# A two-block diffusion layer on one core: decay's scan behind the short convolution, root tables called ahead of the last squares, three row sums, three weight chunks and one load elsewhere

## Chip, cores and metric

One core of a Trainium2 chip runs the whole program in one launch. The time is the device time of one execution in microseconds; three executions of the kernel before took 1831.81, 1833.35 and 1838.54, median 1833.35.

## The reference

A latent sequence `x` of 256 tokens and a context of 256 tokens, 1024 features each, in float32, go through three layers: one block with a gated delta rule, a short convolution and a Fourier branch, then a block with retention and mLSTM, and a block with windowed attention. Each has a SwiGLU network with 2816 hidden features, and every norm is modulated by vectors that come from `c` through a 1024 x 6144 matrix.

```
mod = silu(c) @ w_mod + b_mod                 # six vectors per layer, for x and for the context
h   = rmsnorm(x) * gain * (1 + scale) + shift
qkv, z, ba, sc, fn = split(h @ w_in)
qkv = silu(conv3(qkv)); q, k = l2norm(q), l2norm(k)
g   = cumsum over a chunk of  -exp(a_log) * softplus(alpha + dt_bias)     # "decay"
o   = gated_delta(q, k, v, beta, g)           # both directions, context then latent
y   = gates * (o_branch, sc_branch: sb * conv3(scc * sx), fourier_branch)
x   = x + g1 * (y @ w_o);  x = x + g2 * swiglu(modulate(rmsnorm(x)))
# layer 2: retention and mLSTM mixer;  layer 3: attention, its mod from row sums of ada_w
```

## The kernel before

Tokens lie along the free axis and features along the partitions. Every weight product is made in three passes: ScalarE copies a weight tile to `wh` (the high half, L1685), VectorE or GpSimd subtracts to `wl` (the low half, L2219 and L824), and TensorE multiplies `wh` with the high and the low half of the activations and `wl` with the high half (L949 to L951). A latent tile (256 tokens) is 24 products, a joint tile (512 tokens) 24 longer ones.

**Order.** Each engine runs a list written out by hand, and all follow one plan (`make_plan`): the sequence of 1 MB weight chunks that SyncE loads into three slots `raw`, and of PSUM tiles that take eight banks in turn. SyncE issues chunk n only when chunk n-3 has been read or split (L802 and the waits ahead of it). Only three split tiles (`wh`, `wl`) exist, so `ahead(key)` on ScalarE, VectorE and GpSimd splits at most three tiles in front of the one that TensorE uses. Anything put in front of a split on an in-order engine delays it.

**Decay.** After qkv and the 128 columns `ba`, the stages z, scc, sx, sb and fn follow, four tiles each. ScalarE and VectorE make softplus of `ba` together (`softplus_act`, `softplus_dve`), VectorE makes gain and sign (two instructions from L2377), then `scan_dve` (L751): eight scans over 128 tokens, two directions by four chunks. They give `RM`, which TensorE transposes after the fn tiles. Beside the stages from scc on runs `l2norm`: ScalarE squares a key or query, TensorE sums and ScalarE roots it (L1853), VectorE inverts (L2387), TensorE spreads (L1071), VectorE multiplies (L2392). TensorE meets a spread after every second tile. In the sx stage VectorE also makes the short convolution (L2358 to L2360, L2418), after clearing its pads (L2405).

**Norms.** `behind` squares a residual tile (L1699) as soon as it has been added, while TensorE makes later tiles; after the last square `root` (L1705) takes the square root of the mean, VectorE inverts (L2278), TensorE spreads (L1044) and VectorE and ScalarE scale and shift. Silu, exp, sqrt and the like lie in different tables of ScalarE; a load (ACT_TABLE_LOAD) precedes the first activation that needs another one. The norms are a1, a2 (first layer), b1 (also the first block's final norm, L1986), b1c, b2, c1 and c2; the mLSTM output has a norm of its own per head (L2035).

**Mod.** 48 chunks of modulation weights are multiplied on TensorE (L1003) in groups placed by `mod(count)`, each group followed one call later by its transposes (L1013). In the recurrence of the gated delta rule (four steps s) a group of two comes at level 2 and another behind level 6. Further groups stand behind the last gate tile (2), between `ydn` and `wo` (1) and at the start of ffn0 (3), in front of the spread of a2. The third layer's modulation is not multiplied: 32 units of rows (`rboth`, `rlat`) are loaded beside the chunks of ffn1, and VectorE sums each against `cond` in two instructions (L2265, `row_sums`); the slot is held until the sum is there. `row_chunk` says beside which chunk a unit stands: in 1 to 7, out 0 to 3, in 8 to 15, out 4 to 7, in 16 to 21, out 8 to 10. ffn1's low halves are all made on GpSimd.

**ffn.** For j = 0 to 21 there are two tiles `fa`, `fb` (gate and value), silu on ScalarE, product and split on VectorE; after 8, 16 and 22 of them come eight output tiles `fo`. In ffn0 step 0 is loaded ahead (`load` ... `use`), and its tiles are made in a pair that follows the norm feature tile by feature tile.

Of the kernel before, what the change touches and what calls it, by code (L numbers as in the profile page):

```python
# [30 lines left out]
ALU = mybir.AluOpType  # L31
# [5 lines left out]
KD = D // P  # L37
# [47 lines left out]
def row_chunk(nm, what, i):  # L85

    if nm != "1" or (what, i) == ("in", 0) or (what, i) == ("out", 11):
        return None  # L90
    at = [("in", x) for x in range(1, 8)] + [("out", x) for x in range(4)]
    at += [("in", x) for x in range(8, 16)] + [("out", x) for x in range(4, 8)]
    at += [("in", x) for x in range(16, 22)] + [("out", x) for x in range(8, 11)]
    return at.index((what, i))

# [10 lines left out]
def make_plan():  # L106
# [77 lines left out]

    def rows_mod(c):

        if c is not None:
            chunk("rboth" if c < BOTH else "rlat", c % BOTH)
            chunks[-1]["unit"] = c
# [7 lines left out]
    def ffn(name, early=None):  # L197
        for g, (k0, nk) in enumerate(GROUPS):
            if g == 2 and early:
                norm(early)  # L200
            for j in range(k0, k0 + nk):
                if j == 0:
                    load("ffn_in" + name, 0, [("fa" + name, 0), ("fb" + name, 0)])
                    if name == "0":
                        mod(3)
                    if name == "1":
                        mod(0)
                    spread({"0": "a2", "1": "b2", "2": "c2"}[name])
                    if name == "0":
                        mod(0)  # L210
                    use([("fa" + name, 0), ("fb" + name, 0)])
                else:
                    split("ffn_in" + name, j, [("fa" + name, j), ("fb" + name, j)])
                if g == 2 and early and j == k0:
                    spread(early)
                rows_mod(row_chunk(name, "in", j))
# [41 lines left out]
    for s in range(NC + 1):  # L258
# [36 lines left out]
        for n in two:  # L295
            add("Y", n, LV - 1)
        mod(2)
        for n in two:
# [15 lines left out]
    load("w_o", 0, [("wo", 0), ("wo", 1)])  # L314
    mod(1)
    use([("wo", 0), ("wo", 1)])
# [140 lines left out]
def build(nc, dram, out):  # L457
# [283 lines left out]

    def scan_dve(dve, src, dst, op, start, done):


        V = nc.vector
        for d in range(2):
            rr = slice(32 * d, 32 * d + 32)
            turn = 1 if d == 0 else -1
            for c in range(NC):
                tk = slice(CH * c, CH * c + CH)  # L750
                ins = V.tensor_tensor_scan(dst[rr, tk][:, ::turn], CA("ones")[rr, :], src[rr, tk][:, ::turn], start,  # L751
                                           ALU.mult, op)
        ins.then_inc(sem(done), 1)
        dve.wait_ge(sem(done), 1)

# [157 lines left out]
    def _(pe):  # L913
# [464 lines left out]
        for m in range(KD):  # L1378
# [3 lines left out]
            plain(("ydn", m), lambda k: w[:, 512 * k + o:512 * k + o + P], lambda k: oacc[:, k, :], 4, L)  # L1382
        mod()
        for m in range(KD):
# [287 lines left out]
    def _(act):  # L1672
# [24 lines left out]
        def square(name, k, nm_res, dst=sqh):  # L1697
            for r, cc in nm_res:
                ins = A(dst[:, k, cc], r[:, k, :], ACT.Square)  # L1699
            ins.then_inc(sem(name + "_sq"), 1)  # L1700

        def root(name):
            rows_n = group_rows(name)
# [8 lines left out]
        def behind(name, m, of, nm_res, dst=sqh):  # L1712

            for k in ((m - 2,) if m < KD - 1 else (m - 2, m - 1, m)):
                if k >= 0:
                    evacuated(act, *of(k))
                    square(name, k, nm_res, dst)

        def shift(name, nidx, nm_res):

            lay, sec = nidx // 2, 3 * (nidx % 2)
            for k in range(KD):
                act.wait_ge(sem(name + "_mul"), k + 1)
                for r, cc in nm_res:
# [23 lines left out]
        def ffn(nm, halves, early=None, after=None):  # L1748
            c0 = T - L * halves
            for g, (k0, nk) in enumerate(GROUPS):  # L1750
# [22 lines left out]
                for m in range(KD):  # L1773
# [6 lines left out]
                    if g == 2 and after == "b1":  # L1780
                        for k in ((m - 2,) if m < KD - 1 else (m - 2, m - 1, m)):
                            if k >= 0:
                                evacuated(act, "fo0", 2 * KD + k)
                                final_squares(k)
# [44 lines left out]
        for what in ("z", "scc", "sx", "sb", "fn"):  # L1829
            for i in range(4):  # L1830
# [8 lines left out]
                if what == "z":  # L1839
                    full(act, "z", i)  # L1840
                    free(A(zsave[:, i, :], bank("z", i)[:, 0:L], ACT.Silu), "z", i)
                elif what == "scc":
                    full(act, "scc", i)
# [127 lines left out]
        for k in range(KD):  # L1971
# [3 lines left out]
            A(mgh[:, k, :], merged[:, k, :], ACT.Copy).then_inc(sem("mg_hi"), 1)  # L1975
        mod()
        for m in range(KD):
# [130 lines left out]
        for s in range(NC):  # L2108
# [18 lines left out]
            full(act, "MD", s)  # L2127
            free(A(den[:], bank("MD", s)[:, 0:P], ACT.Abs), "MD", s)
        mod()
        act.wait_ge(sem("mout_sum"), 2)  # L2130
# [79 lines left out]
    def _(dve):  # L2210
# [40 lines left out]

        def row_sums(c):

            if c is None:
                return
            n = unit_at[c]
# [119 lines left out]
        softplus_dve(dve, link, "dsp", r, tmp)  # L2376
        link(V.scalar_tensor_tensor(r[:, 3, :], r[:, 0, :], 0.0, r[:, 3, :], ALU.max, ALU.add))  # L2377
        evacuated(dve, "ba", 0)
        link(V.tensor_scalar(r[:, 0, :], r[:, 3, :], tiny[0:64, 0:1], -1.0, ALU.mult, ALU.mult))
        scan_dve(dve, rows[0:64, 0, :], RM[0:64, :], ALU.add, 0.0, "RM_ready")  # L2380

# [13 lines left out]
        for what in ("z", "scc"):  # L2395
            for i in range(4):
                ahead(what, i)
                if i % 2:
                    if what == "scc":
                        l2norm(i // 2)  # L2400

        pads = [cb[:, i % 3, 0:4 * (GRID + 1) + 1] for i in range(4)]
        dve.wait_ge(sem("conv_done"), 12)
# [3 lines left out]
        for i in range(4):  # L2407
# [12 lines left out]
            if i % 2:  # L2420
                l2norm(2 + i // 2)
        for i in range(4):
            ahead("sb", i)
            full(dve, "sb", i)
            free(V.tensor_tensor(scy[:, i, :], bank("sb", i)[:, 0:L], scy[:, i, :], ALU.mult), "sb", i)
            if i % 2:
                l2norm(4 + i // 2)
        for i in range(4):
            ahead("fn", i)
# [180 lines left out]
        for m in range(KD):  # L2610
            if m == 2:
# [7 lines left out]
                            ALU.subtract).then_inc(sem("mg_split"), 1)  # L2619
        mod()  # L2620
        for m in range(KD):
# [570 lines left out]
```

## Time and profile before

| | us |
|---|---|
| median of three runs | 1833.35 (1831.81 to 1838.54) |
| the profiled execution | 1837.42 |
| its span | 1835.6 |
| TensorE busy | 1720.0 (94%), 14308 products |
| VectorE / ScalarE / GpSimd busy | 938.8 / 733.9 / 592.2 |
| HBM read | 259.44 MB, 142 GB/s over the span |
| mean granted clock | 0.969 |

The profile is one execution of the program. Busy time is the union of an engine's instructions; register, branch and DMA-issuing instructions are not in it. The chain is followed back from the last instruction to what released each one. The granted clock is TensorE's, as a share of full speed.

### The profile page before, as it was taken

The page shows a single profiled execution, that of the slowest core. Times are in us where ns is not written, and L with a number is a line of the kernel's source. Part 1 is how long each engine was busy: PE and PEld are TensorE (multiplying, and loading weights), DVE is VectorE, ACT ScalarE, POOL GpSimd, SP SyncE. Part 2 cuts the span into 40 slices and gives each one's busy share as a digit, 9 for nine tenths or more (in the row PEclk, how much of TensorE's full clock was granted, in tenths as well). Part 3 has the DMA queues.
Part 4 walks back from the last instruction along what each step waited for, and adds up shares of the span by engine and source line. Part 5 has one row for each costly group of instructions (what it writes and reads, how often), then busy time and mean ns, then how long its engine had stood idle before and what let it go on. Part 6 is the DMA issues. An engine that isn't in the chain of part 4 may idle for free.

```text
span 1835.6 us, 33658 instructions
## 1 busy us (share of the span) xinstructions
PE 1720.0 (94%) x14308; PEld 1508.0 (82%) x14308; DVE 938.8 (51%) x1723; ACT 733.9 (40%) x1267; POOL 592.2 (32%) x302
## 2 busy tenths in 40 slices
PE   4997998999989999899999799999999989989998
PEld 1787997888889999697798577888888777689998
DVE  1758126576443333543487626554554546744333
ACT  2463522232345464431555324212212245744443
POOL 0245322121133443214233024444445312134443
PEclk8999999999999999999999899999999989999999
DMA  8433343332464544423220323434545432035553
GB/s 320 190 137 115 116 161 128 141 146 96 169 236 178 185 180 165 157 93 139 81 92 25 116 74 110 152 124 181 186 185 198 153 119 92 2 104 195 184 184 116
DMA packets 37876, 262.66 MB, mean 143 GB/s; under 512 B 4192, under 2 KB 4320, under 8 KB 8416
## 3 DMA queue, kind: packets, MB, share of 16 engines
q1 hardware_dynamic: 37728, 260.51, 38.6%
q8 instruction: 114, 1.87, 0.4%
q14 instruction: 34, 0.28, 0.0%
HBM read 259.44 MB, written 1.05 MB: 142 GB/s over the span
## 4 chain that ended last, share of the span: by engine, by line
PE 82%; DVE 8%; DMA 3%; ACT 3%; issue 2%; POOL 1%; SPq 0%; DVEq 0%; ACTq 0%; POOLq 0%
PE ps L949 20%; PE ps L951 19%; PE ps L950 19%; PE ps L1003 2%; DMA raw<-in_mod 2%; PE ps L978 2%; PE ps L967 1%; PE ps L968 1%; PE ps L969 1%; POOL wl L824 1%; PE ps L1309 1%; PE ps L1104 1%; PE ps L1655 1%; PE ps L1633 1%; PE ps L1027 1%
## 5 line engine op out<-in xcount | busy, mean ns | idle before, releaser
L824 POOL TENSOR_TENSOR wl<-raw,wh 128x1024 fp32r<-128x1024 f32 (+1 forms) x213 | 519.4, 2442 | 995.2 <-ACT wh L1685 995.2
L949 PE MATMUL ps<-h_hi,wh 128*128 128x256 f32 (+1 forms) x1696 | 546.9, 322 | 7.5 <-POOL wl L824 5.6
L950 PE MATMUL ps<-h_lo,wh 128*128 128x256 f32 (+1 forms) x1696 | 542.1, 320 | 0.0
L951 PE MATMUL ps<-h_hi,wl 128*128 128x256 f32 (+1 forms) x1696 | 542.0, 320 | 0.0
L1685 ACT ACTIVATE wh<-raw 128x1024 fp32r<-128x1024 f32 (+1 forms) x330 | 341.7, 1040 | 397.2 <-PE ps L951 256.8
L949 PEld LDWEIGHTS ps<-h_hi,wh 128*128 128x128 f32 x1696 | 324.1, 191 | 34.3 <-POOL wl L824 7.0
L951 PEld LDWEIGHTS ps<-h_hi,wl 128*128 128x128 f32 x1696 | 324.0, 191 | 22.7
L950 PEld LDWEIGHTS ps<-h_lo,wh 128*128 128x128 f32 x1696 | 324.2, 191 | 22.5
L2219 DVE TENSOR_TENSOR wl<-raw,wh 128x1024 fp32r<-128x1024 f32 (+1 forms) x117 | 146.5, 1252 | 210.6 <-ACT wh L1685 210.5
L949 PE MATMUL ps<-gh,wh 128*128 128x256 f32 (+1 forms) x528 | 170.1, 322 | 0.4 <-POOL wl L824 0.4
L951 PE MATMUL ps<-gh,wl 128*128 128x256 f32 (+1 forms) x528 | 168.8, 320 | 0.0
L950 PE MATMUL ps<-gl,wh 128*128 128x256 f32 (+1 forms) x528 | 168.7, 319 | 0.0
L2265 DVE CUSTOM_DVE_ANT_0 cjunk<-raw,cond,small 128x1024 f32<-128x1024 f32 x64 | 139.3, 2213 | 1.9 <-ACT cond L1768 1.9
L2329 DVE TENSOR_TENSOR sil<-ps,sil 128x256 f32<-128x256 f32 (+1 forms) x66 | 33.9, 514 | 194.7 <-PE ps L951 192.3
L949 PEld LDWEIGHTS ps<-gh,wh 128*128 128x128 f32 x528 | 101.0, 191 | 10.0 <-issue 2.0
L951 PEld LDWEIGHTS ps<-gh,wl 128*128 128x128 f32 x528 | 100.9, 191 | 7.1
L950 PEld LDWEIGHTS ps<-gl,wh 128*128 128x128 f32 x528 | 101.0, 191 | 6.9
L1764 ACT ACTIVATE sil<-ps 128x256 f32<-128x256 f32 (+1 forms) x66 | 30.0, 454 | 152.9 <-PE ps L951 150.6
L845 POOL TENSOR_TENSOR d_Xc<-d_Ac,const 128x256 f32<-128x256 f32 x40 | 31.9, 814 | 136.6 <-DVE d_Ac L2514 101.2
L2345 DVE SCALAR_TENSOR_TENSOR res_l<-ps,mods,res_l 128x256 f32<-128x256 f32 x72 | 34.6, 480 | 59.4 <-PE ps L951 59.4
L1003 PE MATMUL ps<-raw,small 128*32 128x256 f32 x768 | 53.5, 419 | 9.9 <-DMA raw<-in_mod 9.5
L1104 PE MATMUL ps<-h_hi,wh 128*128 128x512 f32 (+1 forms) x96 | 40.0, 417 | 17.6 <-DVE h_lo L2305 17.6
(441 smaller groups left out, 2577.0 us busy)
## 6 DMA issues: line engine op xcount, KB each, us to landing
raw<-in_ffn_in SPq DMA_DIRECT2D x66, 1024.0 KB, 4.8
raw<-in_mod SPq DMA_DIRECT2D x48, 1024.0 KB, 5.1
raw<-in_ffn_out SPq DMA_DIRECT2D x24, 1024.0 KB, 4.8
raw<-in_w_in SPq DMA_DIRECT2D x16, 1024.0 KB, 4.8
raw<-in_rlat SPq DMA_DIRECT2D x16, 1024.0 KB, 4.8
raw<-in_w_gate SPq DMA_DIRECT2D x12, 1024.0 KB, 4.8
raw<-in_w_ab SPq DMA_DIRECT2D x12, 1024.0 KB, 4.9
raw<-in_ffn_out SPq DMA_DIRECT2D x12, 768.0 KB, 4.2
```

The source lines that it names most:

```text
L824: nc.gpsimd.tensor_tensor(wl[e % SPLIT][:, 0:entries[e]["words"]], part(e), wh[e % SPLIT][:, 0:entries[e]["words"]].bitcast(F32), ALU.subt ...
L949: nc.tensor.matmul(b[:, cols], wh[e % SPLIT][:, w], xh(k), start=(k == 0), stop=False)
L950: nc.tensor.matmul(b[:, cols], wh[e % SPLIT][:, w], xl(k), start=False, stop=False)
L951: ins = nc.tensor.matmul(b[:, cols], wl[e % SPLIT][:, w], xh(k), start=False, stop=(k == nk - 1))
L978: ins = nc.tensor.matmul(b[:, 0:cols], w(k), rhs(k), start=(k == 0), stop=(k == nk - 1))
L1003: ins = nc.tensor.matmul(b[32 * j:32 * j + 32, 0:256], small[:, o:o + 32], w[:, 256 * k:256 * k + 256], start=(a == 0 and k < 4), stop=(a ...
L1104: nc.tensor.matmul(o, wh[e % SPLIT][:, w], xh(k), start=(k == 0), stop=False)
L1685: A(wh[e % SPLIT][:, 0:x["words"]], part(e), ACT.Copy).then_inc(hi_ready, 1)
L2219: V.tensor_tensor(wl[e % SPLIT][:, 0:entries[e]["words"]], part(e), wh[e % SPLIT][:, 0:entries[e]["words"]].bitcast(F32), ALU.subtract).th ...
L2265: V.tensor_tensor_reduce(cjunk[:, e, :], w, cond[:, v, :], 1.0, S("bmod")[:, 96 + o:97 + o], ALU.mult, ALU.add, mods[:, 2, o, v:v + 1]).th ...
L2329: free(V.tensor_tensor(sil[:, j % 4, c0:T], bank("fb" + nm, j)[:, c0:T], sil[:, j % 4, c0:T], ALU.mult), "fb" + nm, j)
L2345: ins = V.scalar_tensor_tensor(r[:, m, :], bank("fo" + nm, KD * g + m)[:, cc], mods[:, lay, 40 + m, v:v + 1], r[:, m, :], ALU.mult, ALU.add)
```

## The change

It moves work between places and adds seven small activations; what is computed stays the same.

1. *Decay*: the end of softplus and the two instructions behind it stand behind the scc stage; the scans of direction 0 behind the sx stage, those of direction 1 behind the sb stage. Only the last scan signals and is waited for.
2. *Root tables*: `call_root` takes a square root of one column into a spare column, so that the table is in: behind the last silu of z, ahead of the last square of each norm made by `behind` (a2, b2, c1, c2) and of b1, and behind the last denominator of mLSTM.
3. *Row sums*: the units of out 8, 9 and 10 become second units of in 17, 19 and 21.
4. *Mod chunks*: the group behind level 6 has three chunks instead of two in steps s = 1, 2, 3; the group between `ydn` and `wo` is gone, and that of ffn0 has one chunk instead of three.
5. *Load*: step 1 of ffn0 is loaded right behind step 0, ahead of the mod group, and ScalarE calls its first split inside the shift of a2, at feature tile 4.

```diff
 def row_chunk(nm, what, i):
-    if nm != "1" or (what, i) == ("in", 0) or (what, i) == ("out", 11):
-        return None
+    if nm != "1":
+        return ()
     at = [("in", x) for x in range(1, 8)] + [("out", x) for x in range(4)]
     at += [("in", x) for x in range(8, 16)] + [("out", x) for x in range(4, 8)]
-    at += [("in", x) for x in range(16, 22)] + [("out", x) for x in range(8, 11)]
-    return at.index((what, i))
+    at += [("in", x) for x in (16, 17, 17, 18, 19, 19, 20, 21, 21)]
+    return [u for u, place in enumerate(at) if place == (what, i)]
...
                     load("ffn_in" + name, 0, [("fa" + name, 0), ("fb" + name, 0)])
                     if name == "0":
-                        mod(3)
+                        load("ffn_in0", 1, [("fa0", 1), ("fb0", 1)])
+                        mod(1)
...
         for n in two:
             add("Y", n, LV - 1)
-        mod(2)
+        mod(3 if s else 2)
...
     load("w_o", 0, [("wo", 0), ("wo", 1)])
-    mod(1)
     use([("wo", 0), ("wo", 1)])
...
+        def call_root():
+            A(tiny[:, 300 + roots[0]:301 + roots[0]], eps, ACT.Sqrt)
+            roots[0] += 1
...
             for k in ((m - 2,) if m < KD - 1 else (m - 2, m - 1, m)):
                 if k >= 0:
+                    if k == KD - 1:
+                        call_root()
                     evacuated(act, *of(k))
                     square(name, k, nm_res, dst)
...
             for k in range(KD):
+                if (name, k) == ("a2", 4):
+                    ahead("fa0", 0)
                 act.wait_ge(sem(name + "_mul"), k + 1)
...
                     free(A(zsave[:, i, :], bank("z", i)[:, 0:L], ACT.Silu), "z", i)
+                    if i == 3:
+                        call_root()
...
             free(A(den[:], bank("MD", s)[:, 0:P], ACT.Abs), "MD", s)
+        call_root()
         mod()
...
         softplus_dve(dve, link, "dsp", r, tmp)
-        link(V.scalar_tensor_tensor(r[:, 3, :], r[:, 0, :], 0.0, r[:, 3, :], ALU.max, ALU.add))
-        evacuated(dve, "ba", 0)
-        link(V.tensor_scalar(r[:, 0, :], r[:, 3, :], tiny[0:64, 0:1], -1.0, ALU.mult, ALU.mult))
-        scan_dve(dve, rows[0:64, 0, :], RM[0:64, :], ALU.add, 0.0, "RM_ready")
...  # the four z tiles and the four scc tiles with two norms
+        link(V.scalar_tensor_tensor(r[:, 3, :], r[:, 0, :], 0.0, r[:, 3, :], ALU.max, ALU.add))
+        evacuated(dve, "ba", 0)
+        link(V.tensor_scalar(r[:, 0, :], r[:, 3, :], tiny[0:64, 0:1], -1.0, ALU.mult, ALU.mult))
...  # pads, the four sx tiles with the convolution and two norms
+        scan_dve(dve, rows[0:64, 0, :], RM[0:64, :], ALU.add, 0.0, "RM_ready", (0,))
         for i in range(4):
             ahead("sb", i)
...
+        scan_dve(dve, rows[0:64, 0, :], RM[0:64, :], ALU.add, 0.0, "RM_ready", (1,))
         for i in range(4):
             ahead("fn", i)
```

## Rows read from the trace of the kernel before

**Rows 1.** The page: busy time (share of the span) and instructions; the chain by engine.
```profile
PE 1720.0 (94%) x14308; PEld 1508.0 (82%) x14308; DVE 938.8 (51%) x1723; ACT 733.9 (40%) x1267; POOL 592.2 (32%) x302
...
PE 82%; DVE 8%; DMA 3%; ACT 3%; issue 2%; POOL 1%; SPq 0%; DVEq 0%; ACTq 0%; POOLq 0%
```
**Rows 2.** Stretches: length, busy of PE, PEld, DVE, ACT, POOL, granted clock, DMA share, GB/s.
```profile
143.00:150.00 7.00, 0.00 (x0) 0.00 (x0) 6.95 (x9) 1.79 (x3) 4.06 (x2) 0.84 0.41 150
150.00:156.00 6.00, 5.62 (x31) 5.62 (x32) 3.31 (x6) 0.00 (x0) 0.00 (x0) 0.62 0.00 0
156.00:176.00 20.00, 17.90 (x159) 16.83 (x157) 18.90 (x24) 8.36 (x12) 12.95 (x6) 1.00 0.33 110
...
547.00:551.00 4.00, 4.00 (x23) 4.00 (x22) 1.42 (x2) 0.77 (x1) 2.46 (x1) 0.57 0.45 137
...
1444.00:1452.00 8.00, 5.39 (x30) 4.04 (x29) 5.49 (x9) 2.81 (x6) 2.64 (x2) 0.98 0.61 230
1452.00:1456.00 4.00, 4.00 (x12) 3.09 (x12) 0.31 (x2) 0.00 (x0) 1.99 (x1) 0.62 0.64 213
...
289.00:485.00 196.00, 178.18 (x3194) 159.83 (x3193) 123.53 (x334) 64.62 (x137) 42.05 (x44) 0.97 0.34 126
```
**Rows 3.** Timeline of VectorE: start, us, instruction, count.
```profile
139.91 2.52 DVE L2379 TENSOR_SCALAR rows<-rows,tiny 64x512 f32<-64x512 f32 x1
142.47 6.87 DVE L751 TENSOR_TENSOR_SCAN RM<-const_all,rows 32x128 f32<-32x128 f32 x8
...
175.05 0.95 DVE L2387 RECIPROCAL l2c<-l2c 128x128 f32<-128x128 f32 x1
```
**Rows 4.** The scan's line: duration in ns, min/median/max.
```profile
L751 DVE TENSOR_TENSOR_SCAN RM<-const_all,rows x8: 385/389/2484, 142.5 to 149.0; 32x128 f32<-32x128 f32 x8
```
**Rows 5.** Timeline of ScalarE at a2, ffn0, b1 and b2: in brackets the idle time before.
```profile
531.47 0.42 ACT L1699 ACTIVATE sqh<-res_l 128x256 f32<-128x256 f32 x1 [2.26 <-DVE res_l L2624]
531.90 1.28 ACT L1705 ACT_TABLE_LOAD   x1
533.20 0.36 ACT L1705 ACTIVATE rc<-ps,small 64x128 f32<-64x128 f32 x1
...
543.15 1.04 ACT L1685 ACTIVATE wh<-raw 128x1024 fp32r<-128x1024 f32 x1
...
738.88 0.42 ACT L1745 ACTIVATE sqh<-res_l 128x256 f32<-128x256 f32 x1 [0.75 <-DVE res_l L2345]
...
1098.77 0.37 ACT L1705 ACTIVATE rc<-ps,small 128x128 f32<-128x128 f32 x1 [0.55 <-PE ps L1027]
```
**Rows 6.** Chain of waits in mLSTM's head norm: start, us, what.
```profile
1035.94 3.24 PE ps L1003 x32
```
**Rows 7.** Chain of waits in the last output group of ffn1.
```profile
1444.20 4.22 DMA raw<-in_ffn_out
```
**Rows 8.** VectorE, 1362 to 1436 us: groups, busy, mean ns, idle before; durations.
```profile
L2265 DVE CUSTOM_DVE_ANT_0 cjunk<-raw,cond,small 128x1024 f32<-128x1024 f32 x14 | 29.7, 2154 | 0.0
L2329 DVE TENSOR_TENSOR sil<-ps,sil 128x512 f32<-128x512 f32 x6 | 4.2, 692 | 33.8 <-PE ps L951 33.8
...
L2265 DVE CUSTOM_DVE_ANT_0 cjunk<-raw,cond,small x14: 1274/1278/3421, 1365.3 to 1428.5; 128x1024 f32<-128x1024 f32 x14
```
**Rows 9.** Chain of waits in steps 1 and 2 of the recurrence.
```profile
362.91 1.86 PE ps L1003 x32
...
397.76 7.98 DMA raw<-in_mod
...
405.78 1.07 PE ps L1003 x16
```
**Rows 10.** Issues of mod chunks, 398.5 to 399.3 us: time to landing.
```profile
DMA to landing us min/median/max: 8.0/9.4/10.8
```
**Rows 11.** Chain of waits at the start of ffn0.
```profile
536.15 0.65 PE ps L1044 x4
```
**Rows 12.** What TensorE waited for, 530 to 552 us: total, times, longest.
```profile
PE ps L949 <- POOL wl L824: 1.8, 1, 1.8
```

More of the change, by code:

```diff
@@ L183, in mod, with rows_mod @@
         mods[0] += count
-    def rows_mod(c):
-        if c is not None:
+    def rows_mod(units):
+        for c in units:
             chunk("rboth" if c < BOTH else "rlat", c % BOTH)
@@ L211, in ffn @@
                     use([("fa" + name, 0), ("fb" + name, 0)])
+                elif (name, j) == ("0", 1):
+                    use([("fa0", 1), ("fb0", 1)])
                 else:
@@ L740, in softplus_dve, with scan_dve @@
         link(V.tensor_tensor(r[:, 3, :], r[:, 3, :], tmp, ALU.add))
-    def scan_dve(dve, src, dst, op, start, done):
+    def scan_dve(dve, src, dst, op, start, done, directions=(0, 1)):
         V = nc.vector
-        for d in range(2):
+        for d in directions:
             rr = slice(32 * d, 32 * d + 32)
@@ L752, in scan_dve @@
                                            ALU.mult, op)
-        ins.then_inc(sem(done), 1)
-        dve.wait_ge(sem(done), 1)
+        if directions[-1] == 1:
+            ins.then_inc(sem(done), 1)
+            dve.wait_ge(sem(done), 1)
     HALF = (slice(0, 64), slice(64, P))
@@ L1382, in _ @@
             plain(("ydn", m), lambda k: w[:, 512 * k + o:512 * k + o + P], lambda k: oacc[:, k, :], 4, L)
-        mod()
         for m in range(KD):
@@ L1700, in square @@
             ins.then_inc(sem(name + "_sq"), 1)
+        roots = [0]
+        def call_root():
+            A(tiny[:, 300 + roots[0]:301 + roots[0]], eps, ACT.Sqrt)
+            roots[0] += 1
         def root(name):
@@ L1782, in ffn @@
                             if k >= 0:
+                                if k == KD - 1:
+                                    call_root()
                                 evacuated(act, "fo0", 2 * KD + k)
@@ L1975, in _ @@
             A(mgh[:, k, :], merged[:, k, :], ACT.Copy).then_inc(sem("mg_hi"), 1)
-        mod()
         for m in range(KD):
@@ L2128, in _ @@
             free(A(den[:], bank("MD", s)[:, 0:P], ACT.Abs), "MD", s)
+        call_root()
         mod()
@@ L2250, in mod, with row_sums, unit_sums @@
                                                     ALU.add, ALU.mult))
-        def row_sums(c):
-            if c is None:
-                return
+        def row_sums(units):
+            for c in units:
+                unit_sums(c)
+        def unit_sums(c):
             n = unit_at[c]
@@ L2619, in _ @@
                             ALU.subtract).then_inc(sem("mg_split"), 1)
-        mod()
         for m in range(KD):
```

## The prediction

> **What bounds the kernel now.** I read the page's busy shares and its chain first: TensorE is busy 94% of the span and carries 82% of the chain [rows 1]. What can be won is only time in which TensorE waits or runs at half clock, so the next view was the granted clock by stretch, and then, at every place the diff touches, what ended TensorE's wait. The reader is to see two costs there: the wait itself, and the stretch behind it. From 143 to 150 us TensorE does nothing; from 150 to 156 us it works at a granted clock of 0.62, part of it therefore at the lower level of 1.2 GHz; from 156 on it is 1.00 again [rows 2]. The same pair stands at 1444 to 1456 us.
>
> The profiled execution took 1837.4 us, 1.8 more than its span; the median of the three runs is 1833.35, 4.1 lower. I take every saving from the trace and subtract it from the median, since the waits below are orders of work and not disturbances.
>
> **Part 1, the scan of decay.** Before, VectorE finishes softplus, then gain and sign (2.52 us), then eight scans (6.87), ending at 149.34, and only then inverts the first key norm, for which TensorE waits from just before 143 until past 150, about 7.5 us [rows 2, 3]. A scan by itself takes 0.39 [rows 4]; the two long ones, and the 2.52 of an instruction of 64 rows, fall beside GpSimd's subtractions. In the new order norm 0 is inverted while TensorE still makes the last scc tile, norm 1 as soon as it is rooted (144.3), and then follow the two decay instructions (about 3 with one collision) and the three memsets (1.6), so that the convolutions begin near 150 and not at 156.4. The wait of 7.5 goes, and with it the low clock behind it, 6 us at 0.62, about 2 us.
>
> What is late next is VectorE itself. Its four convolutions and two inversions run from 156.4 to 176.0 (18.9 of 20 us busy [rows 2]), and TensorE waits there for norm 3, inverted at 175.05 to 176.0 [rows 3]. So this 19.6 us chain and not the 9.5 us sets the gain. Started at 150 it ends at 169.6 if it loses as much to GpSimd as before (gain 6.4), and near 166 if half of its four collisions of 2.0 each go (gain 10; TensorE's own work since 143 would end about there). I take 7.5. The scans come back in two halves of 4 x 0.39 = 1.6, up to 2 x 2.1 more when blocked, one before the sb multiplies and one before the fn norms. There TensorE works through two tiles of 3 us between any two norms and does not need RM until the transposes behind fn, so they cost nothing; if that cover is gone, 1.6 to 3.7 each.
>
> Trainium skill, "SBUF — State Buffer", section "Who interferes with whom": a VectorE instruction with two SBUF inputs is blocked for the whole of a GpSimd instruction that reads SBUF. The trace agrees for the scan (0.39 alone, up to 2.48 [rows 4]). By that rule every collision stays where GpSimd runs, which speaks for the 6.4 end.
>
> **Part 2, root tables called ahead.** At a2 the last square is followed by a load of 1.28 and then the root [rows 5]. At b2, where the root's table is already in, the root starts 0.55 behind its square (the wait for TensorE's sum), against 1.31 here. A call put behind square 6 runs in ScalarE's wait of 2.3 for the last tile, so a2, c2 and c1 gain 1.31 - 0.55 = 0.76 each. At b1 ScalarE idles only 0.75 before square 7; call and load (1.5) push the squares back 0.7 of the 1.3 saved: 0.6. In mLSTM's head norm the load stands on the chain, TensorE's mod chunks behind it run partly at half clock (3.24 us for two chunks [rows 6], 1.9 elsewhere), and the second chunk's landing limits them; I take 1.9, between 1.3 (the load) and 2.6 (load and clock). At z the call adds 1.5 us to ScalarE and delays one split that GpSimd, busy back to back, would not take earlier: nothing. At b2 it is a 0.2 us activation in a wait. Parts without a2: 0.76 + 0.76 + 0.6 + 1.9 = 4.0; bounds 2.5 and 5.5.
>
> Trainium skill, "ScalarE: Activation LUTs", section "What ACT_TABLE_LOAD costs": a switch costs 1283 ns and a drain of about 1380 behind it. By that figure each place would give nearly twice as much. The trace shows the root 0.02 us behind the load [rows 5], so nothing of a drain is there to save.
>
> **Part 3, three row sums.** In the last output group of ffn1 a sum on VectorE holds a slot, SyncE issues the next weight chunk only at 1444.20 [rows 7], and TensorE works 5.4 of the 8 us from 1444 (2.6 of waiting), then runs 1452 to 1456 at 0.62 [rows 2], 1.7 more. Sums at out 8 to 10 no longer exist, so both go: 4.3. They are added at in 17, 19 and 21. There 14 sums, seven units in 74 us, so one step of 10.6 each, take 2.15 on average, 4.3 a unit, and in six waits VectorE waits 33.8 us for TensorE, 5.6 a step [rows 8]; a second unit leaves 1.3. The two units' slots come free some 4 us later, which the splits, due a step later, can bear. I take a loss of 0.5: net 3.8, bounds 4.3 and -1.
>
> **Part 4, three mod chunks and one load.** In the recurrence TensorE is 91% busy (178.2 of 196 us) at a granted clock of 0.97 [rows 2]. Two chunks take 1.86 [rows 9], so three more cost 2.8. At s = 2 the w_gate chunk holds a slot until GpSimd's split ends, and three chunks are then issued together: the second lands at 405.74, TensorE waits 0.5 for it and is done with it at 406.85; a third issued at 398 to 399 takes up to 10.8 [rows 9, 10], so it lands at 408.5 to 409.7: 2.3 lost, and half a chance of 1.7 of low clock behind it. At s = 1 and 3 the third slot is free long before. Sum: -2.8 - 2.3 - 0.9 = -6.0 (bounds -3, -9). The chunk taken from between ydn and wo gives nothing back: there ScalarE and VectorE split the merged tiles and TensorE waits anyway.
>
> What it buys is the start of ffn0. Now three chunks stand between the sum of a2 and its spread, which runs at 536.15 [rows 11], and the first tile of step 1 waits 1.8 for its split [rows 12], since ScalarE begins that at 543.15 only behind the shift [rows 5]. It then runs at 0.57 clock, 23 products in the 4 us to 551 [rows 2], so that its second tile starts at about 551. New: root at 532.45 and done at 532.8, inverse (0.95) at 533.8, spread at 533.85, 2.3 earlier, a2's table with it. The split called inside the shift, 1.04 us of ScalarE, makes VectorE wait 0.5. Tiles 0, which closed at 544.8, close at 543.0, step 1 begins at once and at full clock, and its second tile waits until about 546.6 for its own split, which stands behind the silu table (1.28), silu (0.4), the high half (1.04) and the low half (1.2), counted from 542.7: against 551 that is 4.5 gained (bounds 2.5 and 6). Part 4: -1.5.
>
> **The sum.** 7.5 + 4.0 + 3.8 - 1.5 = 13.8 us. From the profiled execution 1823.6; from the median 1819.6, so 1820.
>
> **Rivals.**
> *A. VectorE's port (0.20).* The moved chain is blocked as often as before or more often (decay's two instructions, the first half of the scans now ahead of norm 4), gain 4; and double sums run past the step: a sum takes 1.27 alone and up to 3.42 behind a split [rows 8], so four at 3.0 and 1.4 for the gate products come to 13.4 against 10.6. At in 21 the last gate product is then late, a wait of 2.8 plus a clock fall of 1.7 eats part 3. For it: 18.9 of 20 us busy [rows 2]. Against it: 5.6 us of waiting a step [rows 8]. 13.8 - 3.5 - 4 = 6.3: 1827. The page of the skill named in part 1 states the lock that this works by.
> *B. Slower: the third chunk (0.05).* Place: the end of s = 1, 2, 3. If each time it is the last of three in flight, TensorE loses 0.93 + 2.9 and then a stretch of 6.8 us at half clock, 3.4: 7.2 a time, 21.7 in all against the 19.8 that the other terms give: 1835. It decides against the change from 6.6 us a step on. Against it: only s = 2 has the gate chunk in the slot that counts.
> *C. The call doesn't serve (0.07).* If the squares or copies behind it call for another set, the root still loads and ten loads stand where five stood: part 2 and 0.8 of a2 go, 1 us is added: 1825. Against it: at b2 squares and copies lie between two roots with no load [rows 5].
> *D. More (0.18).* VectorE collides half as often (10), no clock falls at s = 2, ffn0 gives 6: 13.8 + 2.5 + 0.9 + 1.5, about 19: 1815.
>
> **How the numbers follow.** The forecast has 0.50, its own range 1816 to 1824. The five cases put 8 in 10 between 1813 and 1829. A measurement of this kernel tells about 0.5% (9.2 us) from no change, so faster means below 1824.2: most of the forecast, all of D, a quarter of A and a third of C, 0.71; same 0.25; slower 0.04.
>
> **What would show it.** Right: no wait of TensorE at 143, one or two of under 4 us between 155 and 167, the transposes behind fn some 7 us earlier; roots 0.55 behind their last square at a2, c1 and c2; no wait in the last output group of ffn1; a wait of 2 to 3 us on a mod chunk at the end of s = 2 and none at s = 1, 3; no wait for the split of step 1 in ffn0. Wrong: the 7.5 us reappear before norm 3 or at the fn norms; loads stand in front of the roots; in21's products are late; or the recurrence stage is over 8 us longer.

## The result, and the profile after

| kernel | median of its runs, us | mean granted clock |
|---|---|---|
| before | 1833.29 (1828.57 to 1838.54, 6 runs) | profiled 0.969 |
| after | 1818.23 (1811.64 to 1823.54, 6 runs) | 0.974 to 0.981 |

The ratio is 0.9908, 95% interval 0.9885 to 0.9931: 15.1 us less in the medians, where 1820 was forecast (a sum of 13.8 less). The profiled execution took 1813.53 us, at the fast end of its six. Two far slower executions further down, of 2800 and 4243 us, are in no median and no comparison.

The page of the kernel after, busy time and chain by engine, answers to [rows 1]:

```profile
PE 1705.2 (94%) x14306; PEld 1496.4 (83%) x14306; DVE 926.7 (51%) x1722; ACT 734.5 (41%) x1273; POOL 590.4 (33%) x302
...
PE 83%; DVE 7%; DMA 4%; ACT 3%; issue 2%; POOL 1%; SPq 0%; DVEq 0%; ACTq 0%; POOLq 0%
```

Span less TensorE's busy time is its waiting: 115.6 us before (1835.6 - 1720.0), 106.5 after (1811.7 - 1705.2). So of the 23.9 us between the two profiled executions only 9.1 are waits; the other 14.8 are nearly the same products done in less time, at a higher granted clock (0.981 against 0.969). How much of that belongs to the change is seen where next to no part of it acts. Stretches of the same 2146 products, from the gates to mLSTM (columns as in [rows 2]), in the kernel before, the kernel after and a second profile of the kernel after:

```profile
800.00:1026.00 226.00, 218.16 (x2146) 189.14 (x2144) 141.03 (x305) 93.56 (x154) 72.05 (x44) 0.98 0.22 78
```

```profile
790.00:1014.50 224.50, 215.87 (x2146) 186.50 (x2145) 141.08 (x305) 94.87 (x156) 72.09 (x44) 1.00 0.22 78
```

```profile
788.50:1016.00 227.50, 219.63 (x2146) 190.16 (x2144) 141.07 (x305) 94.98 (x156) 72.06 (x44) 0.98 0.22 77
```

The wait is 7.8, 8.6 and 7.9 us, but the length 226.0, 224.5 and 227.5: the clock alone makes 1.5 us either way. The next table therefore has two profiles of the kernel after. Each number is how much earlier (-) or later (+) a stretch ends than it began, against the same TensorE products of the kernel before; the stretch is named by its time there. The last column is the profile of the kernel that has only that part.

| stretch (us of before) | forecast | after | after, 2nd | part alone |
|---|---|---|---|---|
| 0 to 120, nothing changed | 0 | -0.2 | -1.9 | |
| 120 to 182, decay and convolution | -7.5 | -8.0 | -7.9 | -8.0 |
| 182 to 286, up to the recurrence | 0 | +0.3 | +0.6 | +0.6 |
| 286 to 484, recurrence | +6.0 | +2.5 | +4.3 | +3.9 |
| 484 to 530, ydn and wo | 0 | +0.3 | -1.6 | -1.2 |
| 530 to 556, a2 and ffn0's start | -4.5 | -3.6 | -3.6 | -2.8 |
| 734 to 800, b1 | -0.6 | -1.3 | -1.3 | -1.3 |
| 800 to 1026, nothing of weight | 0 | -1.5 | +1.5 | -1.5 |
| 1026 to 1056, head norm | -1.9 | -2.6 | -1.1 | -2.8 |
| 1070 to 1106, b2 | 0 | -0.9 | -0.5 | -0.9 |
| 1440 to 1460, last output group of ffn1 | -4.3 | -4.3 | -4.3 | -4.3 |
| 1460 to 1497, c1 | -0.8 | -2.0 | -0.8 | -0.4 |
| 1600 to 1650, c2 | -0.8 | -1.8 | -1.9 | -1.8 |

(In the last column, the rows up to 286 are decay's kernel, those of the recurrence to ffn0 the chunks', ffn1's the sums', and the other rows from b1 to c2 the tables'. The 0.5 forecast as lost at in 17 to 21 is not there: from 1106 to 1440 the lead changes by 0.0 and by -0.3. What is left out, 1497 to 1600, changes by -0.8 and -0.1, with no wait changed.)

The kernels with one part alone are also each other's control, since most of them have no edit in a given stretch. This is how far such unedited stretches move against the kernel before, and what TensorE waits in them before and after:

| stretch | kernels without an edit there | waiting before, after |
|---|---|---|
| 120 to 182 | -0.5, -0.4 | 12.3, 4.8 |
| 286 to 484 | +1.3, -1.3, -1.7 | 17.8, 19.1 |
| 734 to 800, b1 | -0.6, -0.6, +0.8 | 4.7, 4.1 |
| 1070 to 1106, b2 | 0.1 at most | 5.2, 5.2 |
| 1440 to 1460 | +0.1, +0.1, +0.1 | 2.6, 0.0 |
| 1460 to 1497, c1 | 0.0, +0.3, 0.0 | 6.4, 5.7 |
| 1600 to 1650, c2 | 0.0, +0.2, 0.0 | 5.9, 5.1 |

So a row of the first table is safe as it stands for decay and the output group of ffn1. In the recurrence it is good to some 1.5 us, and of b1's 1.3 a half is there without the edit in two kernels of three. At b1, c1 and c2 the waiting fell by 0.6, 0.8 and 0.8, which is the forecast; what the rows show beyond it, and all of b2's 0.9, is clock.

**Decay.** Stretches of the kernel after, against [rows 2]:

```profile
143.00:150.00 7.00, 7.00 (x65) 6.67 (x64) 6.41 (x9) 2.71 (x5) 5.38 (x3) 1.00 0.44 150
150.00:156.00 6.00, 6.00 (x52) 6.00 (x53) 5.75 (x8) 2.88 (x4) 3.60 (x3) 1.00 0.55 178
156.00:168.00 12.00, 9.91 (x76) 9.17 (x75) 11.58 (x17) 2.68 (x5) 6.00 (x3) 0.86 0.24 89
```

VectorE there, against [rows 3], and what TensorE waits for in 150 to 172:

```profile
144.61 2.53 DVE L2418 SCALAR_TENSOR_TENSOR rows<-rows 64x512 f32<-64x512 f32 x1
...
151.48 2.46 DVE L2437 COPY scy<-cy 128x256 f32<-128x256 f32 x1
...
155.34 2.48 DVE L2380 SCALAR_TENSOR_TENSOR cy<-cb,small,cy 128x259 f32<-128x259 f32 x1
...
158.19 0.95 DVE L2403 RECIPROCAL l2c<-l2c 128x128 f32<-128x128 f32 x1
...
164.71 0.95 DVE L2403 RECIPROCAL l2c<-l2c 128x128 f32<-128x128 f32 x1
...
166.13 3.38 DVE L753 TENSOR_TENSOR_SCAN RM<-const_all,rows 32x128 f32<-32x128 f32 x4
```

```profile
PE ps L1074 <- DVE l2c L2403: 2.1, 1, 2.1
```

TensorE works through 143 to 156 at full clock. The wait left is one of 2.1 us at the spread of norm 2, and a lower clock (0.86) stands behind it: VectorE's chain, 11.6 of 12 us busy, is the bound up to there, as forecast. In the convolutions two of its instructions are blocked for about 2 us (2.46 and 2.48) where before there were four, and it inverts norm 3 at 164.71 instead of 175.05: 10.3 earlier, the forecast's upper end for VectorE, of which TensorE, with its wait at norm 2 and its own tiles, turns 8.0 into time.

**ScalarE.** a2 and ffn0, against [rows 5]:

```profile
525.46 0.20 ACT L1708 ACTIVATE tiny<-small 128x1 f32<-128x1 f32 x1
526.40 0.42 ACT L1701 ACTIVATE sqh<-res_l 128x256 f32<-128x256 f32 x1 [0.74 <-DVE res_l L2644]
527.33 0.36 ACT L1714 ACTIVATE rc<-ps,small 64x128 f32<-64x128 f32 x1 [0.51 <-PE ps L1030]
...
532.65 1.04 ACT L1687 ACTIVATE wh<-raw 128x1024 fp32r<-128x1024 f32 x1
...
538.17 1.28 ACT L1777 ACT_TABLE_LOAD   x1
539.46 0.38 ACT L1777 ACTIVATE sil<-ps 128x256 f32<-128x256 f32 x1
```

The root stands 0.51 us behind its square, no load between: the call serves. The load itself is not gone (both kernels have 39 in all), it runs in ScalarE's wait ahead of the square, which still has 0.74 to spare.

**Last output group of ffn1**, stretches that answer to 1444 to 1456 in [rows 2], and the sums at in 16 to 21, against [rows 8]:

```profile
1429.00:1437.00 8.00, 8.00 (x42) 6.00 (x40) 1.18 (x3) 2.41 (x6) 3.69 (x2) 1.00 0.37 124
1437.00:1441.00 4.00, 4.00 (x25) 3.12 (x25) 0.88 (x2) 1.46 (x3) 1.85 (x1) 1.00 0.56 236
```

```profile
L2285 DVE CUSTOM_DVE_ANT_0 cjunk<-raw,cond,small 128x1024 f32<-128x1024 f32 x20 | 32.8, 1679 | 0.4 <-DVE mods L2285 0.3
L2349 DVE TENSOR_TENSOR sil<-ps,sil 128x512 f32<-128x512 f32 x6 | 4.2, 692 | 30.2 <-PE ps L954 30.2
```

The 2.6 us wait and the clock of 0.62 are gone.

**Recurrence**, the whole stage against 289 to 485 in [rows 2], what TensorE waits for at the end of s = 2, and the chain there:

```profile
281.10:479.65 198.55, 179.47 (x3242) 159.97 (x3241) 123.95 (x338) 64.64 (x137) 42.13 (x44) 0.98 0.37 141
```

```profile
PE ps L1006 <- DMA raw<-in_mod: 2.3, 1, 2.3
```

```profile
390.65 10.03 DMA raw<-in_mod
```

The chunk that TensorE waits for lands 10.0 us after its issue, and the wait is 2.3 us. The forecast's 2.3 was to come on top of the 0.5 that the kernel before waits there; here the one wait stands in its place, so that the waiting at this point grew by 1.8.

### The profile page after: what moved, and what is told of

It is laid out like the page before. It is cut to its first block, busy times and chain, and to the rows that moved or that the text cites. A ratio compares the mean times of both kernels' runs of the same rounds, so it can differ in the third digit from the quotient of the medians.

```text
span 1811.7 us, 33659 instructions
## 1 busy us (share of the span) xinstructions
PE 1705.2 (94%) x14306; PEld 1496.4 (83%) x14306; DVE 926.7 (51%) x1722; ACT 734.5 (41%) x1273; POOL 590.4 (33%) x302
## 4 chain that ended last, share of the span: by engine, by line
PE 83%; DVE 7%; DMA 4%; ACT 3%; issue 2%; POOL 1%; SPq 0%; DVEq 0%; ACTq 0%; POOLq 0%
PE ps L952 20%; PE ps L954 20%; PE ps L953 20%; DMA raw<-in_mod 2%; PE ps L1006 2%; PE ps L981 2%; PE ps L970 1%; PE ps L972 1%; PE ps L971 1%; POOL wl L827 1%; PE ps L1107 1%; PE ps L1312 1%; PE ps L1030 1%; PE ps L1657 1%; PE ps L1635 1%
## 5 line engine op out<-in xcount | busy, mean ns | idle before, releaser
L2285 DVE CUSTOM_DVE_ANT_0 cjunk<-raw,cond,small 128x1024 f32<-128x1024 f32 x64 | 130.6, 2077 | 2.3 <-ACT cond L1781 1.9
```

What stands on the lines that cost most here:

```text
L2285: V.tensor_tensor_reduce(cjunk[:, e, :], w, cond[:, v, :], 1.0, S("bmod")[:, 96 + o:97 + o], ALU.mult, ALU.add, mods[:, 2, o, v:v + 1]).th ...
```

## The experiments

**1. The four parts, each alone on the kernel before**, their edits being parts 1, 2, 3, and 4 with 5, of "The change", here by their marking lines:

```diff
+        scan_dve(dve, rows[0:64, 0, :], RM[0:64, :], ALU.add, 0.0, "RM_ready", (0,))
...
+        call_root()
...
+    at += [("in", x) for x in (16, 17, 17, 18, 19, 19, 20, 21, 21)]
...
+        mod(3 if s else 2)
+                        load("ffn_in0", 1, [("fa0", 1), ("fb0", 1)])
```

> The kernel before with the decay part alone. Theory (VectorE's chain through the convolution sets the end): no wait of TensorE at 143 us, one wait of about 2 us near 157, and the spread of norm 3 begins 7 to 9 us earlier than before; behind the sb tiles the lead stays constant up to ffn1. Time about 8 us below the kernel before (ratio 0.9956). Rival (the wait of 7.5 us and the low clock behind it are the whole gain): TensorE is 9 to 10 us ahead from 150 us on and stays so. Rival (the gain in the changed kernel comes from the clock and not from the order): no constant lead behind the sb tiles.

> The kernel before with the seven calls of the root alone. Theory: the root begins 0.55 us behind its last square at a2, c1 and c2 (1.31 before); TensorE gains 0.8 at c1 and at c2, 0.6 at b1, 1.3 to 2.6 in mLSTM's head norm; at a2 nothing or little, since three mod chunks stand in front of the spread; at z nothing. Sum 3.5 to 5 us apart from clock stretches. Rival (a drain behind each load is saved too): 2 us and more at c1 and c2.

> The kernel before with the three moved row sums alone. Theory: the wait of 2.6 us in the last output group of ffn1 and the low clock behind it go, 4.3 us, and no new wait stands in steps 16 to 21 of ffn1. Rival (VectorE is full in the doubled steps): a wait of TensorE on the last gate product behind in 21, up to 2.8 us, or a split in steps 18 and 20 that comes late.

> The kernel before with the three moved mod chunks, the load and the early split call alone. Theory: TensorE loses 2.3 us at the end of s = 2 on the third chunk and up to 0.93 us of work at the end of s = 1, 2 and 3 each, in all 3 to 6; it gains 3 to 4.5 at the start of ffn0, with root's table of a2 still in the way 0.76 less than in the changed kernel. Net between -1 and +3 us: this part alone is not a gain worth measuring. Rival (the parts of ffn0 are a gain by themselves): net 4 us faster.

Measured: decay alone 1827.36 us median (1822.26 to 1832.05, 5 runs) against 1834.84 of before beside it, ratio 0.9952 (0.9932 to 0.9972), 7.5 less. The others ran once: tables 1829.66, sums 1831.14, chunks 1832.38; single times spread by more than these differ, so they are read by the table's last column. Every effect of a part is there in its own kernel, within what unedited stretches scatter, and none needs another part. The expected rival of the tables, a drain saved behind each load, would take 2 us and more at c1 and c2; the waiting fell by 0.8 at each, so it is out, though c2's row with its clock is near it. The chunks' kernel comes out near nothing over its three rows (3.9 - 1.2 - 2.8), as was expected, though ffn0's 2.8 is a little under the 3 to 4.5 named for it. The tables' kernel also shows what the clock does without any longer wait: from 120 to 182 us it loses 2.4 us (its only edit there is the call at z, which the kernel after has too), with the same wait before norm 0 (7.4, before 7.5), at a clock of 0.53 from 150 to 156 where [rows 2] has 0.62, and of 0.72 from 176 to 182 where before has 1.00. In the sums' kernel the last output group of ffn1 has no wait and full clock.

The chunks' kernel waits 2.0 us for the third chunk, until 404.23. The last 1.2 us of that wait and what follows:

```profile
403.00:407.00 4.00, 2.77 (x35) 1.86 (x36) 0.21 (x1) 0.38 (x1) 0.00 (x0) 0.81 0.92 342
```

and its whole recurrence, with that of the sums' kernel, whose recurrence is that of the kernel before:

```profile
284.47:484.33 199.86, 181.17 (x3242) 161.27 (x3241) 123.91 (x338) 64.63 (x137) 42.15 (x44) 0.97 0.37 140
```

```profile
286.95:481.26 194.31, 176.78 (x3194) 158.62 (x3193) 123.43 (x334) 64.68 (x137) 42.11 (x44) 0.98 0.34 128
```

At the same clock of 0.98 the kernel after takes 198.55: 4.2 more than this 194.31, of it 2.7 work (179.47 against 176.78) and 1.5 waiting (19.1 against 17.5).

**2. All scans ahead of the pads.**

```diff
+        scan_dve(dve, rows[0:64, 0, :], RM[0:64, :], ALU.add, 0.0, "RM_ready")
         pads = [cb[:, i % 3, 0:4 * (GRID + 1) + 1] for i in range(4)]
...
-        scan_dve(dve, rows[0:64, 0, :], RM[0:64, :], ALU.add, 0.0, "RM_ready", (0,))
...
-        scan_dve(dve, rows[0:64, 0, :], RM[0:64, :], ALU.add, 0.0, "RM_ready", (1,))
```

> The kernel after, with all eight scans put back in one run directly in front of the pads, behind the scc tiles and norms 0 and 1. TensorE does not need RM before the transposes behind fn in either version. Theory (VectorE's chain through the convolutions sets the end of the stage): the scans, 3.1 us alone and up to 6.9 with collisions (rows 4 of before), delay the four convolutions and with them the inversions of norms 2 and 3, so TensorE's wait for the spread of norm 2 (2.1 us in the kernel after) grows to 5 to 9 us and the stage ends 3 to 7 us later; in the median 1821 to 1825. Rival (what mattered was only that the 7.5 us wait before norm 0 went, VectorE has room behind it): TensorE's wait stays within 0.5 us and the time is that of the kernel after, 1818.

Measured: 1823.74 us, the median of four executions (1817.41 to 1825.32), ratio to before 0.9929 (0.9894 to 0.9963). VectorE, and TensorE's wait:

```profile
148.16 7.03 DVE L753 TENSOR_TENSOR_SCAN RM<-const_all,rows 32x128 f32<-32x128 f32 x8
155.37 1.59 DVE L2425 MEMSET cb<- 128x520 f32 x3 [0.18 <-DVE RM L753]
```

```profile
PE ps L1074 <- DVE l2c L2403: 7.2, 1, 7.2
```

The wait grew from 2.1 to 7.2 us, and TensorE leaves the stage 6.3 us later. Against the kernel before, 1.7 us of the 8.0 are left (TensorE's waiting 9.9 against 4.8 in the kernel after, the rest clock). The theory holds, the rival falls: an early norm 0 alone brings little as long as the scans stand in front of the convolution.

**3. Without the early split of ffn0's step 1.**

```diff
-                if (name, k) == ("a2", 4):
-                    ahead("fa0", 0)
```

> The kernel after, without the split of ffn0's step 1 called inside the shift of a2; the load of step 1 ahead of the mod group and the single mod chunk there stay. It splits the 3.6 us that the start of ffn0 gained into its two causes. Theory (the early split carries part of it): ScalarE begins that split only behind the shift, TensorE waits about 1.8 us for it again as in rows 12 of before and the low clock behind may be longer, 2 to 3.5 us later than the kernel after from 545 us on. Rival (the earlier spread, by two mod chunks fewer, carries all): no wait over 0.5 us for that tile, and the same lead over before at 552 us as in the kernel after.

Measured: 1818.06 us, ratio 0.9909 (0.9875 to 0.9944); the start of ffn0 0.1 us quicker than in the kernel after, if anything. What TensorE waits for at ffn0's start, in the kernel after and without the early split:

```profile
PE ps L1107 <- DVE h_lo L2325: 2.1, 2, 1.4
```

```profile
PE ps L1107 <- DVE h_lo L2323: 1.4, 1, 1.4
PE ps L952 <- POOL wl L827: 0.7, 1, 0.7
```

One wait of 0.7 us takes the place of another: the early split makes VectorE's shift late by what it saves on GpSimd. The rival is right on the time, though not on its sign (a wait of 0.7, where it had at most 0.5). The 3.6 us of that stretch are two chunks fewer, 1.9 of work [rows 9], and 1.5 of waits: before, 1.8 for the split [rows 12], 1.4 for VectorE, 0.6 for a chunk and 0.5 for the sum; after, 2.1 for VectorE, 0.5 for the sum and 0.2 for the spread. Both kernels load step 1 ahead of the mod group, so no run shows what of this is due to that load and what to the two chunks.

**4. The third chunk of s = 2 in s = 1.**

```diff
-                mod(2)
+                mod(3 if s == 1 else 2)
...
-        mod(3 if s else 2)
+        mod(3 if s % 2 else 2)
```

> The kernel after, with the third chunk of s = 2 moved into the level-2 group of s = 1, so that the end of s = 2 has two chunks as before. Theory (the 2.3 us wait at the end of s = 2 is the third of three chunks in flight behind the gate chunk): that wait goes to 0 to 0.5 us, s = 1 gets 0.9 us of work more of which some lies beside waits, net 1.5 to 2.5 us earlier at 485 us. Rival (slot supply of the whole recurrence is short by one chunk, so the wait moves): a wait of 1 to 2.5 us appears at s = 1 or s = 3 or at the next group, and 485 us comes within 0.5 us of the kernel after.

Measured: 1814.54 us median (1813.59 to 1818.65), ratio 0.9882 (0.9856 to 0.9909), against 0.9906 and 0.9908 of the kernel after. The intervals overlap, so the times alone don't tell the two apart; the stage does. Its recurrence:

```profile
282.30:478.75 196.45, 179.56 (x3243) 160.06 (x3242) 124.00 (x339) 64.93 (x137) 42.17 (x44) 0.98 0.38 143
```

and its longest wait on a mod chunk at the end of s = 2:

```profile
PE ps L1006 <- DMA raw<-in_mod: 0.6, 1, 0.6
```

The same work as the kernel after in 2.1 us less; TensorE's waiting over the stage is 16.9 against 19.1, so the wait did not move elsewhere. It is also less than the 17.5 to 18.8 of the four kernels with three chunks fewer there: some of the added work lies beside waits.

**5. A better version?** The kernel of experiment 4, the call of b1 behind square 4 instead of ahead of square 7, and silu's table called behind the roots of a2 and c2:

```diff
                             if k >= 0:
-                                if k == KD - 1:
-                                    call_root()
                                 evacuated(act, "fo0", 2 * KD + k)
                                 final_squares(k)
+                        if m == KD - 2:
+                            call_root()
...
+            if name in ("a2", "c2"):
+                A(tiny[:, 310 + (name == "c2"):311 + (name == "c2")], eps, ACT.Silu)
```

> chunk_to_s1, and besides: the call of the root table at b1 stands behind square 4 instead of ahead of square 7, where ScalarE has an idle 2 us, and a small silu calls its table right behind the roots of a2 and c2, while VectorE inverts. Theory: the 1.5 us wait of TensorE at b1 goes to 0.5, the 0.7 us wait for the split of the value tile at the start of ffn0 and a like one in ffn2 go, which with the chunk gives 3 to 5 us less than the kernel after, 1814 in the median. Rival for the silu calls (the table load of 1.28 us ends behind the inversion of 0.95 us, and delays the copy of the spread): the spread's copy comes 0.3 to 0.5 us late and nothing of the 0.7 us is won. Rival for b1: the eighth square is last anyway and the wait is the sum's and root's, which stays at 1.5 us.

Measured: 1810.43 us, the median of three executions (1808.68 to 1811.73), ratio 0.9855 (0.9825 to 0.9884). It was run again, with a profile, beside the kernel after and a version in which decay's last two instructions stand behind the sx stage and the first scans in the sb stage:

```diff
-        link(V.tensor_scalar(r[:, 0, :], r[:, 3, :], tiny[0:64, 0:1], -1.0, ALU.mult, ALU.mult))
         pads = [cb[:, i % 3, 0:4 * (GRID + 1) + 1] for i in range(4)]
...
                 l2norm(2 + i // 2)
-        scan_dve(dve, rows[0:64, 0, :], RM[0:64, :], ALU.add, 0.0, "RM_ready", (0,))
...
+        link(V.tensor_scalar(r[:, 0, :], r[:, 3, :], tiny[0:64, 0:1], -1.0, ALU.mult, ALU.mult))
...
                 l2norm(4 + i // 2)
+            if i == 1:
+                scan_dve(dve, rows[0:64, 0, :], RM[0:64, :], ALU.add, 0.0, "RM_ready", (0,))
```

> The kernel after itself, in rounds with the two kernels that build on it. Theory: 1818 as before, 0.8 to 1.1% under the kernel before; its single times spread by some 10 us with the mean granted clock. Rival (its lead comes from a chance run of few low-clock stretches): within 0.6% of the kernel before.

> The third chunk of s = 2 at level 2 of s = 1, the call at b1 behind square 4, and silu's table called right behind the roots of a2 and c2; its first profile was useless (a span of 2798 us). Theory: the waits of 2.3 us at the end of s = 2 and of 0.7 us for the value tile of ffn0 are gone, b1's wait goes from 1.5 to about 0.9 us; 3 to 5 us under the kernel after in the profiled executions once their clocks are equal, 1813 to 1815 in the median. Rival (silu's load of 1.28 us delays the copy of the spread, b1's wait stays): only the 2 us of the chunk are won, 1816.

> The kernel just named, and besides decay's two instructions of 64 x 512 (3.0 us in the kernel after) moved from ahead of the pads to behind the sx stage, the scans of direction 0 to the middle of the sb stage. Theory (VectorE's chain through the convolutions still sets the end, as the scans put ahead of the pads showed): norm 2 is inverted 3 us earlier, TensorE's wait of 2.1 us at its spread goes, and with it part of the low clock behind it, 2 to 4 us less than the kernel just named. Rival (VectorE's work before the pads lies in a wait for the first sx tile or for scc, or the moved work delays norm 4 or 5): TensorE's wait stays over 1.5 us or a new one stands at the spreads of norm 4 or 5, and the time is that of the kernel just named within 1 us.

| kernel | median, us | ratio to before (95%) | span, TensorE's waiting |
|---|---|---|---|
| after | 1818.09 | 0.9906 (0.9891 to 0.9921) | 1816.6, 103.9 |
| better version | 1809.77 | 0.9865 (0.9847 to 0.9882) | 1806.9, 100.4 |
| and decay's two moved | 1813.18 | 0.9874 (0.9855 to 0.9893) | 1811.5, 104.5 |

Beside each other the better version is 8.3 us under the kernel after in the medians, with intervals that don't overlap; its earlier 1810.43 is 7.8 under the kernel after's 1818.23, which is from other runs. That is more than the 3 to 5 expected, and the profiles place only half of their difference of 9.7. 4.3 us lie in the recurrence, since the second profile of the kernel after lost not only the wait but also clock behind it (its wait of 2.5 us ends at 399.78):

```profile
399.00:403.00 4.00, 3.22 (x35) 1.75 (x35) 0.00 (x0) 0.38 (x1) 0.00 (x0) 0.65 1.02 420
```

At b1, TensorE's wait for the last square in the kernel after, and in the better version:

```profile
PE ps L1030 <- ACT sqh L1759: 1.5, 1, 1.5
```

```profile
PE ps L1030 <- ACT sqh L1761: 0.7, 1, 0.7
```

that is 0.6 us in the end. The silu calls gave nothing: the load (523.01 to 524.29) does lie beside VectorE's inversion, but TensorE's 0.7 us there are VectorE's, as experiment 3 shows, and not the split's; my reading of that wait before the run was wrong. The other 5 us of the 9.7 between these two profiles lie where the kernels are alike, and no edit can be given them. The last version lost its bet: norm 2's wait is gone, but VectorE is blocked four times in the convolutions and not twice, three of them:

```profile
153.28 2.47 DVE L2380 TENSOR_SCALAR cy<-cb,small 128x259 f32<-128x259 f32 x1
...
160.62 2.38 DVE L2436 COPY scy<-cy 128x256 f32<-128x256 f32 x1
...
164.41 2.48 DVE L2382 SCALAR_TENSOR_TENSOR cy<-cb,small,cy 128x259 f32<-128x259 f32 x1
```

TensorE then waits the same at norm 3:

```profile
PE ps L1074 <- DVE l2c L2405: 2.2, 1, 2.2
```

It left the stage 1.5 us earlier, with the same waiting (4.8 us in both) and no low clock (1.00 against 0.97); in the medians the two versions can't be told apart. The kernel of choice is the better version.

## Why the prediction was right

*Part 1, 7.5 forecast, 8.0 measured three times.* The step that decided it, that VectorE's chain and not the removed wait sets the gain, is shown by experiment 2. The form came as said too: no wait at 143, one under 4 us in its place, the scans free behind the convolution. What decides within its bounds of 6.4 and 10 is how often VectorE is blocked: instructions of 0.3 to 0.5 us take 2.4 to 2.5, four times before, twice after, four times in the last experiment, whose bet they ate. The first half of rival A (a gain of 4 only) falls with this. Not foreseen, and small: in the kernels with part 1 TensorE waits 0.2 to 0.5 us for a low half of VectorE near 244, where the kernel before and that of experiment 2 have no wait, so the scans in two halves may not have come back quite free; the cause was not followed. The Trainium skill ("SBUF — State Buffer", "Who interferes with whom") has VectorE and GpSimd exclude each other for a whole instruction when VectorE's has two SBUF inputs, or is a copy or a tensor-scalar form in a two-port mode. The trace agrees for all three kinds, each beside a subtraction of GpSimd: 2.48 us (two inputs, at 164.41), 2.38 (a copy, 160.62), 2.47 (a tensor-scalar form, 153.28).

*Part 2, 4.0 and a2's 0.8.* The waits came out as forecast: c1 from 2.4 to 1.6, c2 from 2.3 to 1.5 (the root's and inversion's wait ahead of the spread). Beyond the waits the sum had no term for the clock, which gave b1 1.3 for 0.6, c2 1.8 for 0.8 and b2 0.9 for nothing. At b1 the call did delay square 7: TensorE waits 1.5 for it, then 0.4, together 1.9 against 2.6 before; the other 0.6 is clock, and two kernels without the edit have it too. The head norm's 1.9 was right by luck. Before and after (the same 223 products):

```profile
1026.00:1056.00 30.00, 22.28 (x223) 15.17 (x224) 19.11 (x36) 11.23 (x21) 0.00 (x0) 0.83 0.47 176
```

```profile
1014.50:1042.00 27.50, 20.20 (x223) 13.93 (x224) 19.17 (x36) 10.06 (x21) 0.00 (x0) 0.94 0.50 192
```

7.7 us of waiting became 7.3, for the first spread comes 1.3 earlier and the second chunk's landing then costs 1.0, as the forecast feared; what fell is work, 22.28 to 20.20, by the clock, which the forecast had as at most half of it. The mean of the two profiles (2.6 and 1.1) is 1.9 all the same. Rival C is out.

*Part 3, 3.8 forecast, 4.3.* The gain was exact, the loss of 0.5 did not come. The priced step was 2.15 us a sum; twenty sums average 1.68 and take 32.8 us where fourteen took 29.7 [rows 8]. A second unit cost VectorE 1 us and not 4.3. That sums which follow each other fall beside the same few splits would explain it, but was not tested. Rival A's second half (late products at in 21) dies of this, 30.2 us of waiting are left.

*Part 4, the step most off in size: recurrence 6.0, measured 2.5, 3.9 and 4.3.* The work (2.7) came as forecast. The wait was taken as 2.3 on top of the 0.5 that was there, and is 2.3 in its place; and added chunks lie in part beside waits (experiment 4), so that all waiting grew by 1.5 (at equal clock) and not 2.3. The clock behind the wait, put down with half a chance, fell in two of the five profiles that have the third chunk at s = 2. ffn0 gave 3.6, not 4.5: the fewer chunks and the shorter waits ahead of step 1 gave all of it, and the split in the shift, which I thought would let step 1 begin at full clock, bought nothing (experiment 3). At equal clock the recurrence's loss was priced 1.8 too high and ffn0's gain 0.9 too high, so the two errors partly cancel.

*Rival B* (waits at s = 1, 2, 3) is out: only s = 2. *Rival D* came near in the profiled execution alone, and by clock. What the sum lacked, 1.3 us in the median, is within what single runs scatter, and is not explained further. That the total is nearer than its terms is in part luck: the terms missed by 0.5 to 2 us each, in both directions.

## What to carry to other kernels

Before pricing a removed wait, ask which engine's chain ends next: here 9.5 us of wait and low clock bought 8, because VectorE needed the rest; and long work put in front of that chain costs most of its length (7.0 us of scans, 6.3 lost). A table called ahead pays what the load took out of the dependent chain, and no more if a DMA is due right behind. When a bound engine's clock moves, compare kernels stretch by stretch, beside stretches in which nothing was changed (the whole of the waiting scatters too, 106.5 and 103.9 us in two profiles of one kernel), before a microsecond is put down to an edit.

## What was not expected of the hardware

The same kernel's time follows the granted clock: 1811.64 and 1813.53 us at 0.980 and 0.981, 1815.91 at 0.978, and 1820.55 to 1823.54 at 0.974 and 0.975. The clock of a stretch is not fixed by the program (1.00 and 0.98 for the same 2146 products of one kernel). A wait for the third chunk went over into a stretch at a clock of 0.65 (399 to 403 us) in the second profile of the kernel after and of 0.81 (403 to 407) in the chunks' kernel, but of 1.00 (403 to 407) in the first profile of the kernel after, with the same kernel in the first and the last.

The table load had nothing behind it again: silu stands 0.01 us behind its load at 538.17 (1.28), where the Trainium skill ("ScalarE: Activation LUTs", "What ACT_TABLE_LOAD costs") adds a drain of about 1380 ns. The measurement decides.
